# Fourteen feed-forward tiles in seven products instead of twelve, and the feed-forward norm's sums in two other PSUM banks

## The reference, cut to what matters

```python
def _rmsnorm(x, g):
    return x * rsqrt(mean(x * x, axis=-1) + EPS) * g

x = x + _mem_attend(_rmsnorm(x, g_mem_q), mem_k, mem_v, w_mq, w_mo)
h = _rmsnorm(x, g_ffn)
gate_in = h @ w_gate                       # 1024 x 2816
buf = concatenate([prev, gate_in], axis=1)
conv = conv_b
for j in range(3):                         # causal, depthwise, width 3
    conv = conv + conv_w[j] * buf[:, j:j + t]
f = (gelu(conv) * (h @ w_up)) @ w_down
x = x + f
y = _rmsnorm(x, g_final)
```

## Time and profile before

| | |
|---|---|
| median of three runs | 856.56 us |
| profiled execution: time, span | 857.21, 855.3 us |
| TensorE matmul busy | 819.9 us, 96% of the span |
| VectorE busy | 516.2 us, 60% |
| ScalarE busy | 378.5 us, 44% |
| GpSimd busy | 209.2 us, 24% |
| chain of work that ended last | PE 82%, DVE 9%, DMA 4%, ACT 3% |
| mean granted TensorE clock | 0.995 of full speed |

### The profile page before, as it was taken

How to read it: one execution, slowest core, us unless ns; L and a number is a source line. 1 busy time by engine, 2 the same in 40 slices (tenths; PEclk the granted TensorE clock), 3 DMA queues, 4 the chain that set the end, 5 groups by cost and what they waited for, 6 DMA issues and landing times.

```text
span 855.3 us, 17213 instructions
## 1 busy us (share of the span) xinstructions
PE 819.9 (96%) x7366; PEld 776.6 (91%) x7366; DVE 516.2 (60%) x806; ACT 378.5 (44%) x579; POOL 209.2 (24%) x165
## 2 busy tenths in 40 slices
PE   5999999998999998998999899999999999999996
PEld 4989999887989998985599899999999999999995
DVE  6969998898357535112326966876876868210013
ACT  6535414667655324123324744455455466322221
POOL 4100001110550251430035131021022054745430
PEclk9999999999999999999999999999999999999998
DMA  9211212625655394319412223233233241433302
GB/s 332 77 52 50 75 51 99 204 81 172 184 174 157 115 410 144 98 50 369 173 50 87 88 75 102 96 99 106 93 100 124 75 149 50 149 99 100 104 1 100
DMA packets 31293, 104.99 MB, mean 123 GB/s; under 512 B 3930, under 2 KB 7002, under 8 KB 28786
## 3 DMA queue, kind: packets, MB, share of 16 engines
q1 hardware_dynamic: 31218, 103.90, 36.1%
HBM read 96.28 MB, written 6.71 MB: 120 GB/s over the span
## 4 chain that ended last, share of the span: by engine, by line
PE 82%; DVE 9%; DMA 4%; ACT 3%; issue 1%; SPq 1%; POOL 0%; DVEq 0%; ACTq 0%
PE pj L695 14%; PE pj L697 14%; PE pj L696 14%; PE pj L702 4%; PE pj L704 4%; PE pj L703 4%; DMA w_raw<-in 3%; PE aux L702 3%; PE aux L704 3%; PE aux L703 3%; PE aux L695 2%; PE aux L697 2%; PE aux L696 2%; PE pj L1313 2%; PE aux L1244 2%; DVE h_lo L1912 1%
## 5 line engine op out<-in xcount | busy, mean ns | idle before, releaser
L659 POOL TENSOR_TENSOR w_lo<-w_raw,w_hi 128x512 fp32r<-128x512 f32 x110 | 149.5, 1381 | 471.2 <-ACT w_hi L1456 471.0
L695 PE MATMUL pj<-h_hi,w_hi 128*128 128x260 f32 x656 | 188.6, 287 | 12.4 <-POOL w_lo L659 10.0
L697 PE MATMUL pj<-h_hi,w_lo 128*128 128x260 f32 x656 | 185.7, 283 | 0.0
L696 PE MATMUL pj<-h_lo,w_hi 128*128 128x260 f32 x608 | 171.8, 283 | 0.0
L1456 ACT ACTIVATE w_hi<-w_raw 128x1024 fp32r<-128x1024 f32 x80 | 84.6, 1057 | 184.0 <-PE pj L697 147.0
L695 PEld LDWEIGHTS pj<-h_hi,w_hi 128*128 128x128 f32 x656 | 123.9, 189 | 14.9 <-POOL w_lo L659 10.0
L697 PEld LDWEIGHTS pj<-h_hi,w_lo 128*128 128x128 f32 x656 | 123.9, 189 | 0.0
L696 PEld LDWEIGHTS pj<-h_lo,w_hi 128*128 128x128 f32 x608 | 114.8, 189 | 0.3
L659 POOL TENSOR_TENSOR wx_lo<-w_raw,wx_hi 128x512 fp32r<-128x512 f32 x40 | 53.2, 1354 | 117.5 <-ACT wx_hi L1456 117.5
L695 PE MATMUL pj<-h_hi,wx_hi 128*128 128x260 f32 x208 | 59.0, 284 | 1.1 <-DVE h_lo L1912 1.1
L697 PE MATMUL pj<-h_hi,wx_lo 128*128 128x260 f32 x208 | 58.8, 283 | 0.0
(11 more groups left out here) (484 smaller groups left out, 2356.8 us busy)
## 6 DMA issues: line engine op xcount, KB each, us to landing
w_raw<-in SPq DMA_DIRECT2D x126, 512.0 KB, 3.7
caches<-in SPq DMA_DIRECT2D x14, 1024.0 KB, 12.9
vpg<-in SPq DMA_DIRECT2D x16, 256.0 KB, 3.0
kpg<-in SPq DMA_DIRECT2D x12, 256.0 KB, 3.0
x<-in SPq DMA_DIRECT2D x4, 520.0 KB, 7.6
out<-x SPq DMA_DIRECT2D x16, 130.0 KB, 1.9
out<-kT SPq DMA_DIRECT2D x1, 1040.0 KB
far<-in SPq DMA_DIRECT2D x1, 1024.0 KB, 4.8
```

Source lines behind the costliest of these rows:

```text
L659: nc.gpsimd.tensor_tensor(lo[:, part], w_raw[:, raw_of(n) % 4, part], hi[:, part].bitcast(F32), ALU.subtract).then_inc(lo_done, 1)
L695: pe.matmul(out, s_hi, m_hi_, start=first, stop=False)
L696: pe.matmul(out, s_hi, m_lo_, start=False, stop=False)
L697: ins = pe.matmul(out, s_lo, m_hi_, start=False, stop=last)
```

## The change

Three edits. First, `SEVEN` becomes runs of three: 3-5, 7-9, 11-13, 15-17 and the pair 19, 20, which is fourteen tiles; the plain ones are 0, 1, 2, 6, 10, 14, 18 and 21. The orders are written as loops over runs. Second, the norm ahead of the feed-forward part puts its sums in banks 2 and 3 of `aux`, only part 1 of tile 1 waits for the root, and the root moves up on ScalarE. Third, in both `residual` stages `split_low(7)` comes before the low part of block base + 9. The orders at the end are redistributed.

```diff
-    0, 4, 8, 12, 16, 26, 34, 42, 50, 58, 126, 150)
+    0, 4, 8, 12, 16, 26, 34, 42, 50, 58, 130, 154)
-SEVEN = tuple(t for t in range(3, 20) if t % 3 < 2)
+RUNS = tuple((c, tuple(range(c + 1, min(c + 4, FT - 1)))) for c in range(2, FT - 2, 4))
+SEVEN = tuple(t for _, run in RUNS for t in run)
@@ TensorE, plain_block
                 elif t == 1:
-                    pe.wait_ge(root_done, 6)
+                    if part == 1:
+                        pe.wait_ge(root_done, 6)
@@ TensorE, between plain_block(0, 0) and plain_block(0, 1)
-            feature_sums(0, (HALF, HALF)).then_inc(stats_done, 1)
+            feature_sums(2, (HALF, HALF)).then_inc(stats_done, 1)
@@ ScalarE, residual
                     scale_pair(2)
                     scale_pair(3)
+                root(group, halves(rinv[:, :]), sums01 if base < N_MO else sums23, D)
+                if base == N_MO:
                     high_form(2)
                     high_form(3)
                     high(N_GU + 3)
-                root(group, halves(rinv[:, :]), sums01, D)
@@ ScalarE, the feed-forward tiles: for c, run in RUNS
                 last_tap(c)
                 ff_open(c)
...
+                high_seven(run[0], 3)
+                for t in run:
+                    copy_chain(t, 0)
+                    if t > run[0]:
+                        ff_open(t - 1)
+                    if t < run[-1]:
+                        high_seven(t + 1, 0)
+                    else:
+                        high(UNIT[t + 1])
+                    copy_chain(t, 1)
+                    copy_chain(t, 2)
+                    if t < run[-1]:
+                        high_seven(t + 1, 1)
+                        high_seven(t + 1, 2)
+                        last_tap(t)
+                        high_seven(t + 1, 3)
+                    else:
+                        high(UNIT[t + 1] + 1)
+                if run[-1] + 2 in SEVEN:
+                    high_seven(run[-1] + 2, 0)
+            last_tap(FT - 2)
             high(N_DOWN)
-            last_tap(FT - 2)
             ff_open(FT - 2)
-            high_a(8, 12)
+            act.wait_ge(block_done, UNIT[FT - 1])
+            high_a(0, 4)
             high(N_DOWN + 1)
-            high_a(12, 16)
             last_tap(FT - 1)
+            high_a(4, 8)
             ff_open(FT - 1)
+            high_a(8, 16)
             high(N_DOWN + 2)
@@ VectorE, residual
-                    if s >= 6:
+                    if s == 6:
                         low(base + s + 2)
                     if s == 7:
                         split_low(7, gain, at_ + 8)
+                        low(base + s + 2)
                     add_square(j0 + s, s == 0, T, group)
@@ VectorE, the feed-forward tiles: for c, run in RUNS
+                for t in run:
+                    read_first(t)
+                    if t < run[-1]:
+                        low_seven(t + 1, 0)
+                    if t > run[0]:
+                        multiply(t - 1)
+                        if t < run[-1]:
+                            sum_corners(t + 1)
+                    read_mid(t)
+                    if run[0] < t < run[-1]:
+                        sum_rest(t + 1)
+                    if t < run[-1]:
+                        low_seven(t + 1, 1)
+                    read_last(t)
+                    if t < run[-1]:
+                        low_seven(t + 1, 2)
+                        first_taps(t)
+                        low_seven(t + 1, 3)
             first_taps(FT - 2)
             multiply(FT - 2)
-            low_a(8, 12)
+            low_a(0, 4)
             evict_gate(FT - 1)
-            low_a(12, 16)
+            low_a(4, 6)
             first_taps(FT - 1)
+            low_a(6, 12)
             multiply(FT - 1)
-            low_a(16, FT)
+            low_a(12, FT)
```

More of the change, by code:

```diff
@@ L1818, in high_a @@
                     nc.scalar.activation(a_hi(kt), a_raw[:, kt, :], ACT.Copy).then_inc(a_hi_done, 1)
[L1820 to L1823, removed]
             def copy_chain(t, i):
@@ L1831, in copy_chain @@
                                      ).then_inc(ff_copied, 1)
+            last_tap(0)
+            ff_open(0)
+            high(UNIT[2])
+            high(UNIT[2] + 1)
             last_tap(1)
@@ L1835, in _ @@
             ff_open(1)
-            for c in range(2, FT - 2, 3):
-                a, b = c + 1, c + 2
-                if c > 2:
+            for c, run in RUNS:
+                if c > RUNS[0][0]:
                     last_tap(c - 1)
-                high_seven(a, 1)
-                if c > 2:
+                high_seven(run[0], 1)
+                if c > RUNS[0][0]:
                     ff_open(c - 1)
-                high_seven(a, 2)
+                high_seven(run[0], 2)
                 last_tap(c)
@@ L2538, in _ @@
             multiply(1)
[L2539 to L2542, removed]
+            for c, run in RUNS:
+                sum_corners(run[0])
+                if c > RUNS[0][0]:
                     first_taps(c - 1)
-                sum_rest(a)
-                low_seven(a, 0)
-                if c > 2:
+                sum_rest(run[0])
+                low_seven(run[0], 0)
+                if c > RUNS[0][0]:
@@ L2547, in _ @@
                     multiply(c - 1)
-                low_seven(a, 1)
+                low_seven(run[0], 1)
                 evict_gate(c)
-                low_seven(a, 2)
+                low_seven(run[0], 2)
                 first_taps(c)
-                sum_corners(b)
-                sum_rest(b)
+                if len(run) > 1:
+                    sum_corners(run[1])
+                    sum_rest(run[1])
                 multiply(c)
-                low_seven(a, 3)
-                read_first(a)
@@ L2557, in _ @@
[L2557 to L2572, removed]
+                low_seven(run[0], 3)
```

## The result

The changed kernel is slower. Its median is 863.99 us (862.45 to 865.75, 4 runs) against 857.11 (856.26 to 860.05, 4 runs) of the kernel before in the same measurement, ratio 1.0075 with an interval of 1.0045 to 1.0106. Measured again later with more runs it is 861.08 against 857.24, ratio 1.0042 (1.0026 to 1.0058). The forecast was 855.4 us, with a range of 851.4 to 858.0. Five of the later kernels had one execution each that was far longer (904 to 4543 us), which is left out of their medians and ratios. Differences in us are between medians; the ratios, with a 95% interval, are worked out from all the other executions, so the two can differ by about 1 us.

What follows compares the result with a forecast made beforehand. TensorE's matmul count and what ScalarE and VectorE hand over inside a tile bound it. Tiles -2.9, handovers +3.5, root -4.2, split +1.8 and +0.7 gave -1.1: from 856.56 to 855.4 us, range 851.4 to 858.0.

Steps and rivals of the forecast that it cites:

- The end. 0 us, with 1.3 us to spare: Down projection's start: the last hidden-tile low part is ready at 13.8 us, wanted at 15.1, so no cost.
- My rival for the end: GpSimd's turns hold VectorE's last ten low parts, starving the end: +2.2 at half, +5.6 (862) at full; chance 0.11.
- The term, -4.2: Feed-forward norm: TensorE's wait for the root goes whole, 2.9 us of wait plus the half clock behind it.
- The clock rival: Feed-forward norm: waits for h's low part and the sums make the clock fall; price 1.3 us, 856.7; chance 0.20.
- The handovers: Second to third tile of four runs: TensorE waits for ScalarE's copy of bank 0, 0.87 us each, +3.5.
- The price of split_low(7): Sums start later at both residuals: 0.67 us behind w_out, 1.76 ahead of the feed-forward, where add_square takes 1.79.
- The matmuls: Two more tiles of seven products, 84 matmuls instead of 96 each: -2.9 us off TensorE.
- The bound on product 5: In a run's third tile, ScalarE's copy 1 is done 0.1 us before product 5 wants it; nothing added.

Runs made afterwards that it cites:

- the tiles alone: Kernel before with only the fourteen tiles in runs of three and their orders, norm as before: 861.55 against 857.72 us, ratio 1.0046.
- split alone: Kernel before with only split_low(7) moved ahead of the low part of block base + 9: 858.64 against 857.72 us, ratio 1.0014.
- earlier weights: Changed kernel with the third down block's high part made ahead of high_a(8, 16): 860.84 us against 857.72 of the kernel before, ratio 1.0037.
- copy 0 first: Changed kernel with ScalarE's copy of bank 0 of a run's third tile ahead of last_tap and the fourth high part: 862.01 us.
- gaps: Changed kernel with VectorE waiting for its own instruction before each of the hidden tiles' low parts 16 to 19: 862.44 us.
- low part on VectorE: Changed kernel with the third down block's low part made on VectorE, between hidden tiles' low parts 15 and 16: 859.61 us.
- both copies: Changed kernel with, in a run's third tile, copy 0 ahead of last_tap and copy 1 ahead of the next plain tile's high part: 859.10 us.
- split_low back: Changed kernel with split_low(7) back behind the low part of block base + 9: 858.66 us against 857.24 of the kernel before, ratio 1.0016.

## Why the prediction was wrong

**The step that failed** is "The end. 0 us, with 1.3 us to spare". It measured +2.75 (5.37 at the second group of down blocks less 2.61 at the first). I had counted the low parts of the hidden tiles, which were all in time, and not the third down block's weights on GpSimd beside them. The reading behind it was that GpSimd and VectorE take turns. At this place they do not: GpSimd waits for the whole series of VectorE's instructions (5.69 us), and with gaps put into the series it does not (two in 3.75). The Trainium skill ("SBUF — State Buffer", Who interferes with whom) has the blocked engine wait for the whole instruction of the other; here it waited for eight, so the measurement goes further. What decides between a turn and a hold stays open: at 715.48 us of the same trace GpSimd had its turn behind one low part, though VectorE's next followed at once. My rival for the end had the sides reversed, VectorE held by GpSimd. With that low part on VectorE, the wait was gone without any other in its place.

**The root brought less in the median than its term.** The mechanism was right and the wait went whole. The term, -4.2, was read from one execution in which the clock fell behind the wait; alone the edit measured -3.3 (-4.5 to -2.3). Why less is not settled: at the place its trace gains the full 4.2, and the same trace has a fall of the clock at 257 us. The Trainium skill ("TensorE: Matmul & The Clock Gate", Part 1) has the activity window free-running, and the traces agree in so far as the same wait meets the fall at different places. Behind the wait of 2.6 us the clock falls 0.4 us before the wait ends in the trace before and 1.1 us after it has ended in the trace of the tiles alone. That such a wait can stay without the half clock, so that the gain is 2.9, no trace shows; behind the shorter one of 1.6 us (split alone) the clock stayed at 1.00.

**The clock rival was real, and not exclusive.** At the two waits for h and `acc` the clock stayed at 1.00 in four traces with that edit (changed kernel twice, earlier weights, split alone) and fell in four (copy 0 first, gaps, low part on VectorE, both copies): from the sums to tile 1 these take 9.57, 9.46, 8.36 and 9.48 us instead of 6.73, so the fall cost 1.6 to 2.8 us. The wait for the weights does the same: of the six traces that have it, the clock fell behind it in two (copy 0 first, both copies), for 1.4 to 1.5 us. And in the trace with the gaps it fell behind the 0.76 us for `acc` at 335 us. I had given it 1.3 us and 0.20 as an alternative to the forecast, where it is a part of every kernel with the waits, in some of its executions. Six of the 24 executions of the changed kernel and of both copies together lie at 0.990 or below; none of 66 of the kernel before does.

**What was right.** The handovers: 3.5 us at four tiles, each step of the chain to 0.02 us. The price of split_low(7): 0.7 and 1.75, add_square 1.77 where 1.79 was said, -2.4 when it was put back. The matmuls: -2.9. The bound on product 5 (0.1 us to spare) was right too, and I should have said what it means for a repair: that moving copy 0 alone gives nothing.

**The sum by what was measured**: -2.9 + 3.5 - 3.3 + 2.4 + 2.75 = +2.5 us; of the 3.6 us between this and the forecast's -1.1, the end is 2.75. The second measurement has +3.8 (2.2 to 5.0), so 1.3 us have no measured term of their own; falls of the clock of the sizes above are the likely place, and 0.6 for the caches stands in the first trace. The first measurement, +6.9, is from four runs, two of them at a clock of 0.989. How often the clock falls, and where, was not settled, since most executions have no trace.

## What to carry to other kernels

- Fewer matmuls on a full TensorE are worth only what the handovers leave: write the chain behind each accumulated bank, step by step, also for the next copy in line, before and after a reordering. Removing the first late one shows the second.
- Where GpSimd's result is on the path, look at what VectorE issues without a gap at that time, and if both are needed at once try giving the work to one of them.
- Read the size of a wait from several traces: what the clock adds behind it differs from one execution to the next.

## What the runs showed of the hardware that was not expected

- A GpSimd subtraction of 512 columns (1.28 us alone) took 5.69 us beside a series of VectorE subtractions 0.61 us apart, and at another place of the same trace 1.73 us.
- The granted clock fell to 0.50 (1.2 GHz) at 257 to 259 us in three traces, behind waits of 0.97, 1.08 and 1.29 us. It did not in two others behind waits of 1.18 and 1.19 us at the same place (earlier weights, split_low back), nor behind a wait of 1.55 us at 160.8 us in the trace before. In the trace with both copies it stayed at 0.50 for some 6 us with TensorE at work.
